# Attention with its transposes ahead of the scores, and its tail pieces at later heads

## What is computed

```
def diff_attention(q, k, v, lam, lam_init, norm_g, t5_bias):      # per 128-query block
    s = einsum(q, k) * scale + bias                               # two maps, m = 0, 1
    a = softmax(s)
    w = a[0] - lam * a[1]
    o = rms_norm(einsum(w, v), norm_g) * (1.0 - lam_init)

def neighborhood_attention(q, k, v, rpb):
    p = softmax(q . k_window * d ** -0.5 + bias)
    o = p . v_window

h = concatenate([o_diff, o_na]) @ w_out
x = layer_norm(alpha * x + h, ln1_g, ln1_b)
```

## Time and profile before

| what | us |
|---|---|
| median of 3 runs | 3393.82 (3392.39 to 3395.72) |
| the profiled execution | 3396.41 |
| its span | 3394.6 |
| PE busy in the span | 3167.8 (93%) |
| DVE busy | 2480.7 (73%) |
| ACT busy | 1233.7 (36%) |
| POOL busy | 1090.5 (32%) |

### The profile page before, as it was taken

The page is one execution under the profiler, slowest core; times in us unless marked ns, Lnnn a source line. Parts: engine busy times, 40 slices in busy tenths (PEclk is TensorE's granted clock), DMA queues, the critical chain, the costliest instruction groups (busy, mean ns, idle before and its releaser), DMA issues. The chain is left out here.

```text
span 3394.6 us, 48838 instructions
## 1 busy us (share of the span) xinstructions
PE 3167.8 (93%) x16726; PEld 2800.1 (82%) x16726; DVE 2480.7 (73%) x5112; ACT 1233.7 (36%) x1756; POOL 1090.5 (32%) x684
## 2 busy tenths in 40 slices
PE   7988799899899999999889888998999999999996
PEld 6866589898899999988677665898998999998885
DVE  3166389898688878778732654898978888787886
ACT  2365233344333333333223652333433333333332
POOL 0030056400355545433200301572004555454331
PEclk9989899999999999999999998999999999999998
DMA  7651225354999989889675422254569999898995
GB/s 260 139 131 60 89 83 175 134 235 187 364 347 349 347 319 340 308 316 352 218 268 126 113 81 76 97 174 166 193 235 365 360 340 336 317 343 287 338 353 180
DMA packets 334924, 806.17 MB, mean 237 GB/s; under 512 B 39312, under 2 KB 195472, under 8 KB 300208
## 3 DMA queue, kind: packets, MB, share of 16 engines
q1 hardware_dynamic: 258384, 525.31, 45.4%
q0 software_dynamic: 73728, 268.47, 21.2%
q10 hardware_dynamic: 2656, 10.49, 0.8%
HBM read 711.38 MB, written 99.09 MB: 239 GB/s over the span
## 5 line engine op out<-in xcount | busy, mean ns | idle before, releaser
L183 POOL DMA_INDIRECT g_ring<-in_peer_u,g_idx x256 | 365.4, 1427 | 793.8 <-DVE g_ring L193 744.4
L246 PE MATMUL o_bank<-v_hi,w_hi 128*128 128x512 f32 x1536 | 599.4, 390 | 16.5 <-DVE w_lo L1644 16.5
L247 PE MATMUL o_bank<-v_lo,w_hi 128*128 128x512 f32 x1536 | 600.4, 391 | 0.0
L248 PE MATMUL o_bank<-v_hi,w_lo 128*128 128x512 f32 x1536 | 600.2, 391 | 0.0
L183 POOL DMA_INDIRECT g_ring<-in_peer_v,g_idx x256 | 374.7, 1464 | 503.5 <-DVE x_sb L201 448.4
L1629 DVE TENSOR_TENSOR v_lo<-v_raw,v_hi 128x2048 fp32r<-128x2048 f32 x128 | 293.0, 2289 | 137.8 <-ACT v_hi L1564 137.4
L1564 ACT CAST v_hi<-v_raw 128x2048 fp32r<-128x2048 f32 x128 | 244.9, 1913 | 405.7 <-PE o_bank L248 386.4
L246 PE MATMUL h_bank<-x_hi,ws_hi 128*128 128x384 f32 x1152 | 385.7, 335 | 4.5 <-PEq L1312 4.5
L248 PE MATMUL h_bank<-x_hi,ws_lo 128*128 128x384 f32 x1152 | 385.7, 335 | 0.0
L247 PE MATMUL h_bank<-x_lo,ws_hi 128*128 128x384 f32 x1152 | 385.3, 334 | 0.0
L201 DVE SCALAR_TENSOR_TENSOR x_sb<-g_ring,g_h,x_sb 128x1024 f32<-128x1024 f32 x256 | 328.3, 1282 | 53.5 <-DMA g_ring<-in_peer_v,g_idx 36.3
(11 more groups left out here) (197 smaller groups left out, 6055.6 us busy)
## 6 DMA issues: line engine op xcount, KB each, us to landing
ws_raw<-in_uT SPq DMA_DIRECT2D x128, 1024.0 KB, 5.2
v_raw<-in_peer_v SPq DMA_DIRECT2D x128, 1024.0 KB, 6.9
gates_T<-gate_stage SPq DMA_DIRECT2D x12, 4096.0 KB, 12.6
g_raw<-gates_T SPq DMA_DIRECT2D x128, 384.0 KB, 8.9
w_raw<-in_w_in SPq DMA_DIRECT2D x24, 1024.0 KB, 9.2
ws_raw<-hidden_T SPq DMA_DIRECT2D x56, 384.0 KB, 4.7
w_out_half<-in_w_out SPq DMA_DIRECT2D x32, 512.0 KB, 3.5
ws_raw<-in_peer_wq SPq DMA_DIRECT2D x16, 1024.0 KB, 5.6
```

What stands on the lines that cost most here:

```text
L183: nc.gpsimd.indirect_dma_start(out=tail.ring[n % RING][:, :], out_offset=None, in_=table.rearrange("l e d -> (l e) d"), in_offset=bass.Ind ...
L246: nc.tensor.matmul(out, lh, rh, start=start, stop=False)
L247: nc.tensor.matmul(out, lh, rl, start=False, stop=False)
L248: return nc.tensor.matmul(out, ll, rh, start=False, stop=stop)
```

## The change

It has four parts.

1. On PE a head's turn becomes `turn(u)`, `values(u - 2)`, `scores(u + 3)`.
2. The numbers of the tail pieces grow. PE's mul_0 to mul_7 go from 24-27 and 29-32 to 26-29 and 31-34, and the tail's transposes by one. DVE's add_0 goes from 28 to 32 and add_1 from 33 to 37: three heads behind the last quarter of their half instead of one. The reads move by one, sums and gain by two, norm from 37 to 42; ACT's pieces by two, spread by six.
3. `sq`, where ACT writes its squares, and the output of spread leave `heads_outT` for an unused piece of the table buffer `tb`. So the transposed heads wait for the projection that reads the same tile (`hid`) instead of for spread.
4. That piece is 512 columns wide, so ACT's spread becomes two squares of 512 columns, the second waiting for the first, each with its own accumulator; DVE's spread adds the two in one more instruction. ACT's spread also waits for the sums of the next block (`rms_asked`), which read the same piece.

```diff
-        sq = catT[:, 0:DC // 2, :].rearrange("p c (h d) -> p (c h) d", d=HD)
+        squares = tb[:, NDH * T5_W:NDH * T5_W + NDH * HD]
+        sq = squares.rearrange("p (h d) -> p h d", d=HD)
...
-        MULS = {f"mul_{n}": u for n, u in enumerate((24, 25, 26, 27, 29, 30, 31, 32))}
+        MULS = {f"mul_{n}": u for n, u in enumerate((26, 27, 28, 29, 31, 32, 33, 34))}
...
-        DVE_SLOTS = {"read_diff": 18, "read_na": 19, "sums": 20, "gain": 22, "add_0": 28, "add_1": 33, "spread": 35,
-                     "norm": 37}
+        DVE_SLOTS = {"read_diff": 19, "read_na": 20, "sums": 22, "gain": 24, "add_0": 32, "add_1": 37, "spread": 40,
+                     "norm": 42}
...
                 if piece == "square":
                     act.wait_ge(o_read[0], qt + 1)
                     if qt >= 1:
-                        act.wait_ge(spread, qt)
+                        act.wait_ge(rms_asked, qt)
+                    if qt >= 2:
+                        act.wait_ge(spread, 2 * (qt - 1))
...
                     if i == 0:
-                        act.wait_ge(rms_asked, qt + 1)
+                        if qt >= 1:
+                            act.wait_ge(hid, 2 * PIECES * qt)
...
                     else:
                         if qt >= 1:
-                            act.wait_ge(spread, qt)
+                            act.wait_ge(hid, 2 * PIECES * qt)
...
                 if piece == "spread":
                     act.wait_ge(centred, qt + 1)
-                    nc.scalar.activation(catT[:, :, :].rearrange("p a b -> p (a b)"), x[:, qt, :], ACT.Square,
-                                         bias=mv[:, 0:1], accum_out=mv[:, 1:2]).then_inc(spread, 1)
+                    act.wait_ge(rms_asked, min(qt + 2, TT))
+                    for i in range(2):
+                        if i == 1:
+                            act.wait_ge(spread, 2 * qt + 1)
+                        nc.scalar.activation(squares, x[:, qt, i * 512:(i + 1) * 512], ACT.Square, bias=mv[:, 0:1],
+                                             accum_out=mv[:, 1 + i:2 + i]).then_inc(spread, 1)
...
                 if piece == "spread":
-                    dve.wait_ge(spread, qt + 1)
+                    dve.wait_ge(spread, 2 * (qt + 1))
+                    chain.done(nc.vector.tensor_scalar(mv[:, 1:2], mv[:, 1:2], mv[:, 2:3], None, ALU.add))
+                    chain.wait()
...
+                if u < UNITS:
+                    turn(u)
+                if u >= BEHIND:
+                    values(u - BEHIND)
                 if u + AHEAD < UNITS:
                     scores(u + AHEAD)
-                if u >= BEHIND:
-                    values(u - BEHIND)
-                if u < UNITS:
-                    turn(u)
```

More of the change, by code:

```diff
@@ L602, in attend @@
         catT = m.sb("heads_outT", [P, DC, P])
-        sq = catT[:, 0:DC // 2, :].rearrange("p c (h d) -> p (c h) d", d=HD)
+        squares = tb[:, NDH * T5_W:NDH * T5_W + NDH * HD]
+        sq = squares.rearrange("p (h d) -> p h d", d=HD)
         st = m.sb("ln_sums", [P, 2])
-        mv = m.sb("ln_mv", [P, 2])
+        mv = m.sb("ln_mv", [P, 3])
         rs = m.sb("ln_rs", [P, 2])
@@ L631, in attend @@
         WO_AT = 8
-        MULS = {f"mul_{n}": u for n, u in enumerate((24, 25, 26, 27, 29, 30, 31, 32))}
-        PE_SLOTS = {"turn_na": 20, "turn_diff": 23, **MULS}
-        ACT_SLOTS = {"square": 18, "turn_na": 21, "turn_diff": 24, "spread": 33}
-        DVE_SLOTS = {"read_diff": 18, "read_na": 19, "sums": 20, "gain": 22, "add_0": 28, "add_1": 33, "spread": 35,
-                     "norm": 37}
-        POOL_SLOTS = {"sums": 20, "spread": 35}
+        MULS = {f"mul_{n}": u for n, u in enumerate((26, 27, 28, 29, 31, 32, 33, 34))}
+        PE_SLOTS = {"turn_na": 21, "turn_diff": 24, **MULS}
+        ACT_SLOTS = {"square": 20, "turn_na": 23, "turn_diff": 26, "spread": 39}
+        DVE_SLOTS = {"read_diff": 19, "read_na": 20, "sums": 22, "gain": 24, "add_0": 32, "add_1": 37, "spread": 40,
+                     "norm": 42}
+        POOL_SLOTS = {"sums": 22, "spread": 40}
         SP_SLOTS = {f"mul_{n}": MULS[f"mul_{n}"] for n in range(PIECES)}
```

## The result

| | before | with the change |
|---|---|---|
| median, us | 3393.4 (3392.39 to 3395.72, 6 runs) | 3371.42 (3369.57 to 3373.93, 6 runs) |
| ratio | | 0.9935, interval 0.9922 to 0.9948 |
| the profiled execution | 3396.41 | 3373.93 |
| its span | 3394.6 | 3372.1 |
| attention stage, layer 1 and 2 | 207.6, 207.6 | 199.4, 194.2 |

The forecast was 3371.2 us in a range of 3359 to 3392. The profiled execution is 22.5 us shorter (forecast 22.6), and 8.2 + 13.4 = 21.6 us of that are in the two attention stages. That the median comes within 0.2 us is luck: neither layer saved the 11.3 us of the sum, and several of its terms are off by 1 to 3 us in opposite directions (see the table of terms).

A forecast was written before the change was run, and what follows sets the result against it. The bound alternates: PE in projection stretches, DVE in free stretches. Per layer 6.3 + 2.3 + 1.9 - 0.5 - 0.7 + 2.8 - 0.75 = 11.3 us, 22.6 for two layers, giving a median of 3371.2 us, range 3359 to 3392.

The forecast's parts named there:

- the sum: All predicted savings and losses of one layer's attention stage added up: 11.3 us saved, 22.6 us for two layers.
- opening and first tail: Heads before the first projection: waits for mixed heads grow, 0.7 us lost in the opening and 0.5 in the first tail.
- three add_0: DVE's waits for the projection before add_0, and PE's behind them, vanish: 2.1 us each, 6.3 a layer; DVE's waits under 12.
- two free stretches: Stretches without projection, DVE 90 percent busy: 19.7 and 19.3 us fall to 17.4, saving 2.3 and 1.9 us.
- gap at the end: PE's idle time before the stage's last projection falls from 9.2 to 6.4 us, 2.8 us saved.
- last projection and split square: After the last add nothing hides spread's two squares and DVE's extra addition: 0.75 us lost a layer.
- The order on PE: Transposes first on PE: a few tenths of a us lost per pair of heads without projection cover, nothing under one.
- walked free stretch: Eight heads between projections followed by semaphores: PE waits 0.2, 0.7, 0.5, 1.3 and 0.9 us, stretch 17.4 us.
- Rival 2: Each of 22 differential heads without a quarter around it exposes its mixing, 26.4 us a layer: 3402 us; chance 0.12.
- Rival 1: Only the add_0 waits and the end improve; free stretches stay 19.7 and 19.3 us: 3379.6 us; chance 0.20.
- Rival 3: PE's clock stays up over the shorter gap before the last projection, 3.0 us more saved a layer: 3365 us; chance 0.12.
- Rival 4: No change: free stretches stay, and opening and first tail each lose 3 us more: 3391.6 us; chance 0.10.

## Why the prediction was right, point by point

Layer 1 of the profiled execution, us saved; layer 2 where it differs. The stretches are those of the earlier trace rows and of the table above; the change starts its projections two heads later, so 3.2 us of heads go from behind to in front.

| term | predicted | layer 1 | layer 2 |
|---|---|---|---|
| opening and first tail | -1.2 | 56.6 + 3.2 - 63.7 = -3.9 | +0.5 |
| three add_0 | 6.3 | 1.8 + 1.6 + 1.8 = 5.2 | |
| two free stretches | 4.2 | 2.5 + 2.1 = 4.6 | |
| gap at the end | 2.8 | 9.2 - 6.2 = 3.0 | 2.6 |
| last projection and split square | -0.75 | 22.7 - 23.4 = -0.7 | +0.6 |
| sum | 11.3 | 8.2 | 13.5 (the stage: 13.4) |

**The adds** behaved as read: DVE's wait fell under the 12 us named, and PE's waits behind it went. The term was 1.1 us too high because I priced the pause at 2.1 us each: 1.8, 1.6 and 1.8 were there. What the sum did not say, and the runs with closer adds show, is that the distance carries the free stretches as well: taking it away costs 11.2 us a layer, against 6.3 + 4.2 = 10.5 predicted for these terms together. The reads and norm moved, but with the adds close the free stretches are 19.8 and 19.0 us, as good as those before.

**The order on PE.** I took a few tenths a pair where nothing covers it and nothing under a projection. In the walked free stretch the waits were 0.2, 0.7, 0.5, 1.3 and 0.9, 3.6 in sum; measured 0.61, 0.69, 1.25 and 0.53, 3.1, for a stretch of 17.2 where 17.4 was forecast. The wait of 0.5 at head 24, behind the squares on ACT, has no row. Mis-sized was the layer's total of waits for mixed heads, 16.5 us and not about 8: I had summed the free stretches and the first tail, and the opening adds about as much again. It is no loss of that size, since PE's 15.3 us of waits for maxima went for it. The test of the order by itself gave the surprise: nothing with the change's slots, 33 us lost with the old ones, 10 us lost with norm and spread late. With the adds close in the new places it lost nothing (3392.88 and 3394.0 us). Rival 2 (waits at every uncovered head, over 20 us of them) did not happen in the change, but with the new order and the old places there are 28.0 us of such waits. They are not where the rival had them: 8.0 us are in the projection stretches, where it had none, 10.4 in the free ones (5.1 in the change), and 9.6 ahead of the first quarter (11.4 in the change). So a quarter beside the head is no cover in itself. Which of the old places makes the new order so costly was not tested; add_0 one head behind its quarter does not do it alone.

**Opening and first tail.** -1.2 was forecast. -3.9 in layer 1 is, as I read it, mostly the granted clock (204.40 to 214.60 above: 0.50 while PE was busy throughout); in layer 2, and in both layers of the change run again (58.9 and 59.4 us against 59.8), it gained 0.4 to 0.9. So this term was mis-sized by about 2 us, and outside that one layer it had the wrong sign. That DVE would have held PE there under either order is my reading, and no run took the opening by itself; the order alone began its first quarter no later than the kernel before.

**The end.** 6.2 us in layer 1 and 6.6 in layer 2 for 6.4, the power 1.64 as counted. Waits for the halves of spread in front of gain, which would have shown the forecast wrong from 2 us on: DVE is free at 347.62 and would have got the power's result at 349.34; it began gain at 349.73, so spread held it some 0.4 us.

**The other rivals.** Rival 1 (free stretches stay 19.7 and 19.3) fell with their 17.2 us. Rival 3 (the clock stays up over the shorter gap) came about in part. The clock did fall, but around the start of the last projection it was down for 7.0 us in every layer with the change, and for over 10 us in both layers before. The first 16 products took 10.08 us in layer 1, where the low stretch began only 0.8 us ahead of them, and 8.72 in layer 2, with 8.70 and 8.54 in the change run again, where more of it fell into the gap; 7.03 is full speed. So 1.4 to 1.6 us of the rival's 3.0 came in three layers of four, and make the 0.6 in the table. Rival 4 needed losses of 3 us each in opening and tail that weren't there.

## What to carry to other kernels

An instruction that waits for another engine costs its own wait and then the lead that its engine had: place it by how long its input takes (three heads here instead of one and two, worth 11 us a layer), and price the stretch behind it too. What the new order on the other engine cost depended on the places of the other pieces, and by no rule that these runs show: 33 us with the old places, nothing with the change's or with its adds close, 10 us with norm and spread late. So test the order again after every change of places. Pieces that nobody waits for (norm, spread) belong where another engine is the bound, and not where their own engine is.

## What the chip showed that I had not expected

The same kernel's first layer took 199.4 us in one execution and 193.7 in another. The first has a stretch of 10.2 us at a granted clock of 0.50, from 28 us into the stage, in which PE was busy without a break, right behind two waits of 1.79 and 1.61 us; the second one of 7.0 us, from 21 us on:

```profile
196.00:203.00 7.00, 6.28 (x24) 5.28 (x25) 4.19 (x12) 3.08 (x8) 6.41 (x7) 0.52 0.11 29
```

Up to the first quarter the two layers of one execution differ by 63.7 - 59.3 = 4.4 us. The run with norm alone late shows the same: 62.9 us in the layer where the clock is down for some 14 us from 22 us on, and 59.3 in the one where it is down for 7.0. No run holds the clock fixed, so that it accounts for the whole difference is not shown. That is as much as several terms of the sum, so a stage is compared over both layers and more than one profile.
